# The RWKV gate's eight tiles moved to the wait for the first inverses, with x kept in DRAM meanwhile

## The chip, the cores and the metric

The kernel runs on one core of a Trainium2 chip (TensorE, VectorE, ScalarE, GpSimd and SyncE, which issues most transfers). The metric is the device time of one execution in microseconds, the median of several runs. In the profile PE is TensorE's matmul, PEld its weight load, DVE VectorE, ACT ScalarE, POOL GpSimd, SP SyncE; L2908 is line 2908 of the kernel.

## What is computed

Two blocks of layers over one sequence of 512 tokens with 1024 features: a block of two attention mixers, then a block with an RWKV-7 mixer, a convolutional FFN, windowed attention and a second FFN. All in float32. The change is in the RWKV mixer and its surroundings. Cut to what matters:

```
xr, xw, xk, xv, xa, xg = [x + xx * mu[i] for i in range(6)]
g = sigmoid(xg @ g1) @ g2                       # the gate: 160 features -> 1024
...
S = S * d_t + (S a_t) b_t + v_t k_t ; y_t = S r_t   # a scan over 512 tokens, 16 heads of 64
y = ((y - mean) * rsqrt(var + GN_EPS)) * gn_g + gn_b
bonus = sum(r_h * k_h * r_k, axis=-1, keepdims=True) * v_h
y = y + bonus
mixer = (y * g) @ w_o
x = x + rms_norm(mixer, norm_g[0, 1])
```

## The kernel before

The work is a list of stages, and in each stage every engine has its own stream of instructions, tied by semaphores. `RwkvProject` makes the projections, `RwkvCore` the scan, and an `Output` stage multiplies the core's result with the gate, projects it with `w_o` and adds it to x. At the end of the core all engines wait for each other (`end_stage`).

The residual x rests in SBUF in `env.x`, 4 tiles of 128 tokens x 1024 (2 MB), through the whole kernel. It isn't touched between the norm ahead of the projection and the additions of the `Output` stage (L956).

The core works on eight eighths n = 0 to 7: token tile c = n mod 4, and head group n // 4 (8 heads each). Its work on TensorE is a written-out list, `self.order`: a key such as `("Y", 0)` stands for one step of one eighth. TensorE takes the keys in that order; each key has two of the eight PSUM banks by its place modulo four, and waits until the engine named in `engines` ("A" is ScalarE, "D" VectorE) has taken the result of the key four places before it. ScalarE and VectorE go through the same list and take the keys that are theirs. For one eighth `G1` and `G2` are products that VectorE masks (L3125), `TA` and `Z` are taken by ScalarE, `Y` (L2942) and `OFF` (L2949) put together the inverse of a triangular matrix, and then come `SA0`, `U0`, `S0`, `SA1`, `U1`, `S1` (the state, two chunks of 64 tokens), `R` and `y`, and `T` (L2923), a transpose after which VectorE centres the result (L3091 to L3093). ScalarE squares it (L3012), VectorE reduces the squares (L3100, L3101, a reciprocal), ScalarE takes the root (L3019) and VectorE scales (L3108).

The inverses of 32x32 blocks are made on VectorE by `inverse`, 31 steps of two instructions (L3072, L3074), once for n = 0 to 3 and once for 4 to 7. The first begins in the projection and runs on between VectorE's other work in the core; its result goes to DRAM and is gathered back into another layout by `gather` on SyncE's queue, and `Y` of eighth 0 waits for that. VectorE starts the second inverse once it has `S0` of eighth 0.

The gate is made of eight tiles `("gate", k)`, each of two matmuls of 512 columns: 128 rows of `g2` with `sg[:, 0]` (L2908), and the other 32 rows with `sg[0:32, 1]` (L2909). `sg` is there since the projection. Each float32 matmul shows as two pieces in the profile. In the kernel before they stand at the end of the list, two of them ahead of `T` of eighth 7, and are copied by ScalarE (L3005) into `self.gate`, which is the memory of `k`, needed to the end of the scan.

GpSimd makes the bonus (L3198: v times the bonus of its head; L3200: plus `gn_b`) in the place of v, for one token tile c after another, each followed for c < 3 by the gain (L3204) and the addition (L3207) once VectorE has scaled that tile; for c = 3 VectorE does these two (L3174, L3176). It starts behind `turn` (L3132), which VectorE takes in eighth 6.

Of the kernel before, what the change touches and what calls it, by code (L numbers as in the profile page):

```python
# [7 lines left out]
ALU = mybir.AluOpType  # L8
# [89 lines left out]
class Env:  # L98
# [6 lines left out]
    def __init__(self, nc, ctx, io):  # L105
# [72 lines left out]
        self.stored = self.sem("stored")  # L178
        self.x_added = self.sem("x_added")
# [582 lines left out]
class Output(Stage):  # L762
# [3 lines left out]
    def __init__(self, env, w_out, g_row, oT, o=None, z=None, kd=KD, following=None, before=None, rows=None):  # L766
        super().__init__(env)
        self.rows = rows
        self.o, self.oT, self.kd, self.g_row, self.z = o, oT, kd, g_row, z
        self.before = before  # L770
        self.n = env.outs
        env.outs += 1
        self.ot0, self.tmp0, self.tr0 = env.ots, env.otmps, env.trs
        if o is not None:
            env.trs += KD
            env.ots += KD
        if z is not None:
            env.otmps += KD
        self.lds, self.g0 = load_tokens(env, w_out, 0, D, kd)
        self.y = env.big.rearrange("p (t d) -> p t d", t=NT)  # L780
# [146 lines left out]
    def vector(self, dve, step):  # L927
# [14 lines left out]
        dve.wait_ge(env.g_arrived, 16 * (self.n + 1))  # L942

# [132 lines left out]
class NsaCompressed(Stage):  # L1076


    def __init__(self, env, m, setup, project):
# [23 lines left out]
        self.cmp_ready, self.keys_ready, self.values_ready = env.sem("cmp_ready"), env.sem("cmp_keys_ready"), env.sem("cmp_values_ready")  # L1103
# [5 lines left out]
        self.zeroed = env.sem("cmp_zeroed")  # L1109
# [7 lines left out]
    def tensor(self, pe):  # L1117
# [69 lines left out]
        pe.wait_ge(self.keys_ready, 1)  # L1187
        scores(0)
        for i in range(NT):
# [5 lines left out]
            if i:  # L1195
                pe.wait_ge(self.pT_taken, i)
            else:
                pe.wait_ge(self.values_ready, 1)
# [63 lines left out]
    def vector(self, dve, step):  # L1262
# [25 lines left out]
        for kv in range(2):  # L1288
# [4 lines left out]
                              env.ps[:, 4, 0:GROUPS * NC].rearrange("p (g c) -> p g c", c=NC)).then_inc(self.keys_ready, 1)  # L1293
# [3 lines left out]
        cp.then_inc(self.values_ready, 1)  # L1297
# [1054 lines left out]
class RwkvMemory:  # L2352


    def __init__(self, env):
# [43 lines left out]
        self.bonus_rows = env.take(T, at=slot(6))  # L2399

# [10 lines left out]
        self.gate = self.k  # L2411
# [3 lines left out]
class RwkvProject(Stage):  # L2415
# [229 lines left out]
    def scalar(self, act, step):  # L2645
# [29 lines left out]

        step(nc.scalar.activation(m.keep, env.vec[:, V_B + 24:V_B + 32], ACT.Copy, scale=-1.0, bias=1.0))
# [86 lines left out]
class RwkvCore(Stage):  # L2763
# [11 lines left out]
    def __init__(self, env, m):  # L2775
# [20 lines left out]
        self.order += [("Y", 0), ("OFF", 0)]  # L2796
# [13 lines left out]
        self.order += [("gate", 0), ("gate", 1), ("T", last)] + [("gate", k) for k in range(2, KD)]  # L2810
# [192 lines left out]
    def scalar(self, act, step):  # L3003
# [18 lines left out]
        for key in self.order:  # L3022
# [10 lines left out]
            elif name == "gate":  # L3033
                cp = copy(m.gate[:, n, :], ps[:, 0, :])
# [22 lines left out]
            if name == "gate" and n in (1, 2, 4):  # L3057
                {1: root, 2: square, 4: root}[n](last - 1 if n == 1 else last)
# [20 lines left out]
    def vector(self, dve, step):  # L3079
# [96 lines left out]
        v.tensor_tensor(o, o, m.v[:, NT - 1, :].rearrange("p (k f) -> p k f", f=P), ALU.add)  # L3176

    def gpsimd(self, pool, step):
# [15 lines left out]
        for c in range(NT):  # L3194
            self.wait_ready(pool, "y", NT + c)
            added = m.v[:, c, :]
            heads = added.rearrange("p (h d) -> p h d", d=DH)
            tt(heads, heads, m.bonus[:, c, :].unsqueeze(2).to_broadcast([P, RH, DH]), ALU.mult).then_inc(self.bonus_added, 1)  # L3198
            pool.wait_ge(self.bonus_added, c + 1)
            tt(added, added, m.gn[:, 1, :], ALU.add).then_inc(self.added_ready, 1)  # L3200
            if c < NT - 1:
                pool.wait_ge(self.scaled, NT + c + 1)
                o = m.o[:, c, :, :]
                tt(o, o, m.gn[:, 0, :].rearrange("p (k f) -> p k f", f=P), ALU.mult).then_inc(self.gained, 1)  # L3204
                pool.wait_ge(self.gained, c + 1)
                pool.wait_ge(self.added_ready, c + 1)
                step(tt(o, o, added.rearrange("p (k f) -> p k f", f=P), ALU.add))  # L3207
# [58 lines left out]
def build(nc, io, out):  # L3266
    with ExitStack() as ctx:
# [28 lines left out]
            Output(env, io["w_o_rwkv_2"][0], g[0, 1], rm.oT, rm.o, rm.gate, following=(g[0, 2], fm.u)),  # L3296
# [19 lines left out]
        for stage, after in zip(stages, stages[1:]):  # L3316
            if isinstance(after, DiffProject):
                stage.ahead = after.k[:3]
            elif isinstance(after, RwkvProject):
                stage.shifted, after.norm = after, stage.norm  # L3320
# [75 lines left out]
```

## Time and profile before

| | |
|---|---|
| median of 3 runs | 2237.29 us (2236.55 to 2238.26) |
| span of the profiled execution | 2243.0 us (no other time of it is shown) |
| mean granted clock of TensorE | 0.936 of full speed |
| busy: PE, DVE, ACT, POOL | 92%, 38%, 41%, 41% |
| chain that ended last, by engine | PE 80%, DVE 9%, ACT 3%, POOL 3%, issue 3%, DMA 1% |
| projection, core and output stages around the change | the projection from about 789, the core from about 1043.7, the output stage from 1257.2 us of the span |

Times of rows are microseconds from the start of the span. The granted clock is TensorE's, where 1.00 is 2.4 GHz and 0.50 is 1.2 GHz.

### The profile page before, as it was taken

To read this page: it belongs to the slowest core of one execution; us is meant where nothing else is said; L and a number is where in the kernel's file an instruction comes from. 1 tells how busy PE (TensorE), PEld (TensorE's weight loads), DVE (VectorE), ACT (ScalarE), POOL (GpSimd) and SP (SyncE) were. 2 spreads that over 40 slices of the span, in tenths; PEclk is the share of its full clock that TensorE was granted. 3 is DMA by queue.
4 is the path that set the end of the run, shared out by engine and by line. 5 is a ranking of instruction groups with operands and counts; after the bars stand their busy time and mean duration, and the time that the engine had idled before them with its cause. 6 is when DMAs were issued, how large, how long until landed. Compare 5 with 4: busy or idle time off the path is not lost.

```text
span 2243.0 us, 33578 instructions
## 1 busy us (share of the span) xinstructions
PE 2074.1 (92%) x13582; PEld 1666.0 (74%) x13582; DVE 846.6 (38%) x1809; ACT 927.9 (41%) x1702; POOL 915.1 (41%) x636
## 2 busy tenths in 40 slices
PE   6999899999997888997588999999998999999998
PEld 5898766788865755876577588888887678888887
DVE  2100567230037456057565443334024535334301
ACT  3331477453246544343123354444234645444412
POOL 3332267534456322241012725445434552444542
PEclk9987899999998978898579899999999999999999
DMA  4222100223310221221210223333322122333332
GB/s 146 79 70 76 48 11 2 66 69 94 94 47 29 62 61 41 77 68 41 50 29 19 94 66 94 94 99 109 105 82 76 48 76 65 95 102 96 104 108 80
DMA packets 222393, 161.05 MB, mean 72 GB/s; under 512 B 30663, under 2 KB 205327, under 8 KB 222240
## 3 DMA queue, kind: packets, MB, share of 16 engines
q1 hardware_dynamic: 220048, 151.83, 22.8%
q0 software_dynamic: 2192, 7.07, 1.1%
q8 instruction: 109, 1.79, 0.3%
q14 instruction: 44, 0.36, 0.1%
HBM read 153.64 MB, written 5.24 MB: 71 GB/s over the span
## 4 chain that ended last, share of the span: by engine, by line
PE 80%; DVE 9%; ACT 3%; POOL 3%; issue 3%; DMA 1%; POOLq 1%; SPq 0%; DVEq 0%; PEld 0%; PEldq 0%; ACTq 0%
PE ps L386 15%; PE ps L348 13%; PE ps L350 13%; PE ps L359 13%; PE ps L396 8%; PE ps L1413 2%; PE ps L1426 2%; PE ps L1402 2%; POOL weights_lo L289 1%; DVE ps L949 1%; DVE buffer L956 1%; POOLq L3261 1%; PE ps L1140 1%; PE ps L2965 1%; PE ps L2202 1%
## 5 line engine op out<-in xcount | busy, mean ns | idle before, releaser
L289 POOL TENSOR_TENSOR weights_lo<-buffer,weights_hi 128x1024 fp32r<-128x1024 f32 (+1 forms) x265 | 654.4, 2471 | 981.1 <-ACT weights_hi L278 980.9
L278 ACT ACTIVATE weights_hi<-buffer 128x1024 fp32r<-128x1024 f32 (+1 forms) x265 | 276.2, 1045 | 339.5 <-PE ps L396 284.7
L348 PE MATMUL ps<-u_hi,weights_hi 128*128 128x512 f32 (+1 forms) x752 | 279.3, 379 | 5.6 <-DVE u_lo L703 3.0
L350 PE MATMUL ps<-u_lo,weights_hi 128*128 128x512 f32 (+1 forms) x736 | 274.8, 377 | 0.0
L2000 ACT ACTIVATE buffer<-ps,buffer 128x512 f32<-128x512 f32 x88 | 68.7, 781 | 276.3 <-PE ps L359 276.3
L359 PE MATMUL ps<-u_hi,weights_lo 128*128 128x512 f32 (+1 forms) x752 | 176.5, 377 | 0.0
L2030 DVE SCALAR_TENSOR_TENSOR buffer<-ps,buffer,buffer 128x511 f32<-128x511 f32 x88 | 66.0, 750 | 287.8 <-ACT buffer L2000 287.8
L348 PEld LDWEIGHTS ps<-u_hi,weights_hi 128*128 128x128 f32 x752 | 142.0, 191 | 31.9 <-issue 5.6
L350 PEld LDWEIGHTS ps<-u_lo,weights_hi 128*128 128x128 f32 x736 | 138.4, 188 | 25.5
L359 PEld LDWEIGHTS ps<-u_hi,weights_lo 128*128 128x128 f32 x752 | 136.3, 190 | 25.8
L3005 ACT ACTIVATE buffer<-ps 32x256 f32<-32x256 f32 (+5 forms) x96 | 47.8, 499 | 158.3 <-PE ps L2965 68.3
L386 PE MATMUL ps<-weights_hi,act_hi 128*128 128x512 f32 x352 | 108.8, 390 | 0.5 <-issue 0.5
L386 PE MATMUL ps<-weights_hi,act_lo 128*128 128x512 f32 x352 | 108.4, 389 | 0.0
L1488 POOL TENSOR_SCALAR buffer<-buffer,buffer,buffer 128x512 f32<-128x512 f32 (+3 forms) x128 | 76.8, 612 | 40.8 <-DVE buffer L1368 40.0
L396 PE MATMUL ps<-weights_lo,act_hi 128*128 128x512 f32 x352 | 92.8, 389 | 0.0
L948 DVE RECIPROCAL buffer<-buffer 128x1 f32<-128x1 f32 x24 | 3.9, 161 | 229.5 <-ACT buffer L865 229.5
L348 PE MATMUL ps<-nsa_u_hi,weights_hi 128*128 128x512 f32 x192 | 83.4, 434 | 4.2 <-DVE nsa_u_lo L703 2.4
L1447 ACT ACTIVATE buffer<-buffer,buffer 128x512 f32<-128x512 f32 (+3 forms) x128 | 71.4, 558 | 30.2 <-DVE buffer L1521 29.1
L350 PE MATMUL ps<-nsa_u_lo,weights_hi 128*128 128x512 f32 x192 | 81.3, 424 | 0.0
L348 PE MATMUL ps<-diff_u_hi,weights_hi 128*128 128x512 f32 (+1 forms) x216 | 77.6, 373 | 3.3 <-ACT weights_hi L278 2.2
L386 PEld LDWEIGHTS ps<-weights_hi,act_hi 128*128 128x128 f32 x352 | 65.7, 188 | 15.4 <-issue 2.1
L386 PEld LDWEIGHTS ps<-weights_hi,act_lo 128*128 128x128 f32 x352 | 66.1, 188 | 13.8
(403 smaller groups left out, 4268.2 us busy)
## 6 DMA issues: line engine op xcount, KB each, us to landing
buffer<-in_w_up SPq DMA_DIRECT2D x88, 512.0 KB, 3.8
buffer<-in_w_down SPq DMA_DIRECT2D x44, 512.0 KB, 3.4
buffer<-in_diff_w_in SPq DMA_DIRECT2D x32, 512.0 KB, 4.0
buffer<-in_nsa_w_in SPq DMA_DIRECT2D x28, 512.0 KB, 3.8
buffer<-in_w_rkv SPq DMA_DIRECT2D x24, 512.0 KB, 4.0
buffer<-in_nsa_w_out SPq DMA_DIRECT2D x8, 512.0 KB, 3.6
buffer<-in_diff_w_out SPq DMA_DIRECT2D x8, 512.0 KB, 3.5
buffer<-in_w_o_rwkv SPq DMA_DIRECT2D x8, 512.0 KB, 3.5
```

The lines of the kernel that those rows point to most:

```text
L278: self.nc.scalar.activation(self.part_hi[:, part % self.PARTS, 0:n], self.raw[:, ld % self.RAW, 0:n], ACT.Copy).then_inc(self.hi_ready, 1)
L289: self.nc.gpsimd.tensor_tensor(self.part_lo[:, part % self.PARTS, 0:n], self.raw[:, ld % self.RAW, 0:n], self.part_hi[:, part % self.PARTS ...
L348: nc.tensor.matmul(out, hi[:, k, :], rhs[0][:, k, tokens], start=(k == 0), stop=False)
L350: nc.tensor.matmul(out, hi[:, k, :], rhs[1][:, k, tokens], start=False, stop=False)
L359: mm = nc.tensor.matmul(out, lo[:, k, :], rhs[0][:, k, tokens], start=False, stop=(k == KD - 1))
L386: nc.tensor.matmul(out(i, b), lhs[part][:, index * m + k, i * P:(i + 1) * P], hi[:, k, b * width:(b + 1) * width], start=(index + k == 0 a ...
L396: mm = nc.tensor.matmul(out(i, b), lhs[0][:, index * m + k, i * P:(i + 1) * P], lo[:, k, b * width:(b + 1) * width], start=False, stop=stop)
L1447: nc.scalar.activation(m.p[:, at, 0:n], m.p[:, at, 0:n], ACT.Exp, scale=-1.0, bias=m.nmax[:, at:at + 1], accum_out=m.psum[:, at:at + 1]).t ...
L1488: nc.gpsimd.tensor_scalar(p, p, m.scale[:, at:at + 1], m.gate[:, i, gate:gate + 1], ALU.mult, ALU.mult).then_inc(self.p_scaled, 1)
L2000: nc.scalar.activation(m.conv[:, 2 * (j % 2) + half, :], env.bank(g), ACT.Identity, scale=self.col(2, half, j), bias=self.col(3, half, j)) ...
L2030: step(nc.vector.scalar_tensor_tensor(c[:, 1:T], env.bank(g)[:, 0:T - 1], self.col(1, half, j), c[:, 1:T], ALU.mult, ALU.add))
L3005: copy = lambda dst, src: nc.scalar.activation(dst, src, ACT.Copy)
```

## The change

- The eight `gate` tiles move from the end of the order to the wait for the first inverses: tiles 0 to 3 behind `TA` of eighth 1, then `Z` of eighth 1, then tiles 4 to 7, and behind them `Y` of eighth 0. `T` of eighth 7 is then the last key.
- `self.gate` is no longer the memory of `k`, which is in use then, but that of `env.x`. ScalarE stores x to a DRAM tensor at the start of the projection in one transfer, and waits for it before it copies a gate tile. In the `Output` stage ScalarE loads it back in four transfers, each behind the second of the two gate tiles in its place, and VectorE waits for them ahead of its first addition to x.
- The bonus of token tiles c = 2 and 3 is made right behind `turn`, ahead of c = 0, into free memory (`late`) and not in the place of v, which the scan still reads.
- ScalarE's last root and square steps follow the list, where they followed certain gate tiles.
- In an earlier stage (`NsaCompressed`) two semaphores, `keys_ready` and `values_ready`, become one that counts to 1 and 2, and an unused one goes.

```diff
+        self.x_spilled = self.sem("x_spilled_and_back")
+        self.x_dram = nc.dram_tensor("x_kept", (P, NT * D), F32, kind="Internal").ap()
...
@@ Output.scalar
             nc.scalar.activation(self.oT[0][:, k, :], self.turned(k), ACT.Copy).then_inc(env.oT_hi_ready, 1)
+            if self.x_kept and k % 2:
+                act.dma_start(env.x[:, k // 2, :], env.x_dram[:, k // 2 * D:(k // 2 + 1) * D]).then_inc(env.x_spilled, 16)
...
@@ Output.vector
         dve.wait_ge(env.g_arrived, 16 * (self.n + 1))
+        if self.x_kept:
+            dve.wait_ge(env.x_spilled, 16 * (1 + NT))
...
@@ RwkvMemory
+        late = env.take(2, D, at=slot(6))
+        self.added = [self.v[:, 0, :], self.v[:, 1, :], late[:, 0, :], late[:, 1, :]]
...
-        self.gate = self.k
+        self.gate = env.x.rearrange("p i d -> p (i d)").rearrange("p (k t) -> p k t", k=KD)
...
@@ RwkvProject.scalar
+        env.wait_x(act, self.x_of, NT - 1)
+        act.dma_start(env.x_dram, env.x.rearrange("p i d -> p (i d)")).then_inc(env.x_spilled, 16)
...
@@ RwkvCore.__init__
         self.order = [(name, 0) for name in first] + [("dg", n) for n in range(NT, 2 * NT)] + [(name, 1) for name in first]
-        self.order += [("Y", 0), ("OFF", 0)]
+        self.order[-1:-1] = [("gate", k) for k in range(4)]
+        self.order += [("gate", k) for k in range(4, KD)] + [("Y", 0), ("OFF", 0)]
...
-        self.order += [("gate", 0), ("gate", 1), ("T", last)] + [("gate", k) for k in range(2, KD)]
+        self.order.append(("T", last))
...
@@ RwkvCore.scalar
             elif name == "gate":
+                act.wait_ge(env.x_spilled, 16)
                 cp = copy(m.gate[:, n, :], ps[:, 0, :])
...
-            if name == "gate" and n in (1, 2, 4):
-                {1: root, 2: square, 4: root}[n](last - 1 if n == 1 else last)
+        root(last - 1)
+        square(last)
+        root(last)
...
@@ RwkvCore.gpsimd
-        for c in range(NT):
-            self.wait_ready(pool, "y", NT + c)
-            added = m.v[:, c, :]
-            heads = added.rearrange("p (h d) -> p h d", d=DH)
-            tt(heads, heads, m.bonus[:, c, :].unsqueeze(2).to_broadcast([P, RH, DH]), ALU.mult).then_inc(self.bonus_added, 1)
-            pool.wait_ge(self.bonus_added, c + 1)
-            tt(added, added, m.gn[:, 1, :], ALU.add).then_inc(self.added_ready, 1)
...
+        self.wait_taken(pool, "gate", KD - 1)
+
+        def add_bonus(n, c):
+            heads = lambda x: x.rearrange("p (h d) -> p h d", d=DH)
+            tt(heads(m.added[c]), heads(m.v[:, c, :]), m.bonus[:, c, :].unsqueeze(2).to_broadcast([P, RH, DH]),
+               ALU.mult).then_inc(self.bonus_added, 1)
+            pool.wait_ge(self.bonus_added, n + 1)
+            tt(m.added[c], m.added[c], m.gn[:, 1, :], ALU.add).then_inc(self.added_ready, 1)
+
+        add_bonus(0, 2)
+        add_bonus(1, 3)
+        for c in range(NT - 1):
+            if c < 2:
+                self.wait_ready(pool, "y", NT + c)
+                add_bonus(2 + c, c)
```

## Rows read from the trace of the kernel before

**Rows 1.** Chain that ended last, around the first `Y`: start us, us, what

```profile
1080.44 1.89 DMA buffer<-inverses_turned
1082.47 1.08 PE ps L2942 x32
...
1092.34 0.04 DVE buffer L3156
```

**Rows 2.** Timeline ahead of the first `Y`: start us, us, what, idle before

```profile
1062.53 1.19 DVE L2885 COPY buffer<-ps 32x128 f32<-32x128 f32 x4
...
1070.16 1.97 PE L2934 MATMUL ps<-buffer,buffer 64*64 64x64 f32 x32 [7.32 <-DVE buffer L3125]
```

**Rows 3.** Windows: stretch, us, busy per engine, PEclk, DMA share, GB/s

```profile
1059.80:1063.70 3.90, 1.94 (x8) 1.57 (x8) 3.65 (x12) 0.83 (x1) 0.00 (x0) 0.50 0.00 0
1082.40:1107.00 24.60, 18.23 (x351) 17.01 (x353) 7.98 (x23) 5.16 (x12) 0.00 (x0) 0.50 0.10 17
892.60:900.20 7.60, 7.20 (x9) 2.58 (x9) 6.04 (x7) 4.14 (x7) 3.18 (x2) 0.50 0.00 0
900.20:902.60 2.40, 2.40 (x6) 1.92 (x7) 0.00 (x0) 0.69 (x1) 0.00 (x0) 0.50 0.47 126
1230.50:1237.20 6.70, 6.70 (x112) 5.52 (x110) 3.11 (x6) 1.92 (x4) 3.06 (x2) 0.50 0.01 4
1237.30:1254.00 16.70, 16.66 (x36) 4.81 (x34) 14.07 (x12) 5.00 (x11) 14.86 (x7) 1.00 0.00 0
```

**Rows 4.** Timeline of TensorE: the nearest prices of a gate tile and of `Y`

```profile
893.00 7.19 PE L2475 MATMUL ps<-buffer,buffer 64*128 64x512 f32 x8 [1.52 <-ACT buffer L2708]
...
1236.09 1.68 PE L2908 MATMUL ps<-buffer,buffer 128*128 128x512 f32 x2
...
1238.75 1.13 PE L2908 MATMUL ps<-buffer,buffer 128*128 128x512 f32 x2
...
1198.89 0.69 PE L2942 MATMUL ps<-buffer,buffer 32*32 32x32 f32 x32
```

**Rows 5.** Timeline of GpSimd in the tail of the core

```profile
1221.99 2.35 POOL L3204 TENSOR_TENSOR buffer<-buffer,buffer 128x1024 f32<-128x1024 f32 x1 [13.93 <-DVE buffer L3108]
...
1239.74 1.90 POOL L3198 TENSOR_TENSOR buffer<-buffer,buffer 128x1024 f32<-128x1024 f32 x1
...
1241.72 2.34 POOL L3200 TENSOR_TENSOR buffer<-buffer,buffer 128x1024 f32<-128x1024 f32 x1
...
1252.64 3.20 POOL L3200 TENSOR_TENSOR buffer<-buffer,buffer 128x1024 f32<-128x1024 f32 x1
```

**Rows 6.** Timeline of VectorE, and `T` 7 on TensorE, in the tail

```profile
1209.15 0.17 DVE L3101 TENSOR_SCALAR buffer<-buffer 128x8 f32<-128x8 f32 x1
...
1219.69 0.69 DVE L3091 TENSOR_REDUCE buffer<-ps 128x8 f32<-128x512 f32 x1 [3.04 <-PE ps L2923]
...
1221.23 0.68 DVE L3108 TENSOR_TENSOR buffer<-buffer,buffer 128x512 f32<-128x512 f32 x1
...
1237.56 2.13 DVE L3101 TENSOR_SCALAR buffer<-buffer 128x8 f32<-128x8 f32 x1
...
1240.86 0.66 PE L2923 MATMUL ps<-buffer,buffer 128*128 128x128 f32 x4
...
1248.41 2.40 DVE L3108 TENSOR_TENSOR buffer<-buffer,buffer 128x512 f32<-128x512 f32 x1 [0.31 <-ACT buffer L3019]
...
1250.84 2.81 DVE L3174 TENSOR_TENSOR buffer<-buffer,buffer 128x1024 f32<-128x1024 f32 x1
...
1255.95 1.23 DVE L3176 TENSOR_TENSOR buffer<-buffer 128x1024 f32<-128x1024 f32 x1 [2.30 <-POOL buffer L3200]
```

**Rows 7.** Timeline at the projection's head, and windows behind it and in the output

```profile
791.22 1.23 ACT L2657 ACTIVATE mix_w_hi<-buffer 128x512 fp32r<-128x512 f32 x2 [1.90 <-DVE buffer L2570]
...
794.00:818.00 24.00, 20.04 (x49) 10.19 (x50) 21.05 (x31) 11.95 (x19) 2.35 (x1) 0.65 0.00 0
...
1264.60:1298.00 33.40, 33.40 (x160) 27.66 (x159) 6.62 (x9) 10.13 (x13) 19.29 (x11) 1.00 0.35 112
```

More of the change, by code:

```diff
@@ L762, with __init__ @@
 class Output(Stage):
-    def __init__(self, env, w_out, g_row, oT, o=None, z=None, kd=KD, following=None, before=None, rows=None):
+    def __init__(self, env, w_out, g_row, oT, o=None, z=None, kd=KD, following=None, before=None, rows=None, x_kept=False):
         super().__init__(env)
+        self.x_kept = x_kept
         self.rows = rows
@@ L1102, in __init__ @@
             env.release(self.w1[2 * kv + 1], self.hid_ready, kv + 1)
-        self.cmp_ready, self.keys_ready, self.values_ready = env.sem("cmp_ready"), env.sem("cmp_keys_ready"), env.sem("cmp_values_ready")
+        self.cmp_ready, self.keys_then_values = env.sem("cmp_ready"), env.sem("cmp_keys_then_values")
         self.bias_ready, self.bias_taken = env.sem("cbias_ready"), env.sem("cbias_taken")
@@ L1108, in __init__ @@
         self.o_ready, self.o_taken = env.sem("co_ready"), env.sem("co_taken")
-        self.zeroed = env.sem("cmp_zeroed")
         self.tensor_goes_on = True
@@ L1186, in tensor @@
         project(3)
-        pe.wait_ge(self.keys_ready, 1)
+        pe.wait_ge(self.keys_then_values, 1)
         scores(0)
@@ L1197, in tensor @@
             else:
-                pe.wait_ge(self.values_ready, 1)
+                pe.wait_ge(self.keys_then_values, 2)
             for g in range(GROUPS):
@@ L1292, in vector @@
         nc.vector.tensor_copy(m.kcmp[:, :, 0:NC],
-                              env.ps[:, 4, 0:GROUPS * NC].rearrange("p (g c) -> p g c", c=NC)).then_inc(self.keys_ready, 1)
+                              env.ps[:, 4, 0:GROUPS * NC].rearrange("p (g c) -> p g c", c=NC)).then_inc(self.keys_then_values, 1)
         for j in range(HPG):
@@ L1296, in vector @@
                                        env.ps[0:NC, 5, 0:GROUPS * DH].rearrange("p (g d) -> p g d", d=DH))
-        cp.then_inc(self.values_ready, 1)
+        cp.then_inc(self.keys_then_values, 1)
         take(0)
@@ L3175, in vector @@
         dve.wait_ge(self.added_ready, NT)
-        v.tensor_tensor(o, o, m.v[:, NT - 1, :].rearrange("p (k f) -> p k f", f=P), ALU.add)
+        v.tensor_tensor(o, o, m.added[NT - 1].rearrange("p (k f) -> p k f", f=P), ALU.add)
     def gpsimd(self, pool, step):
@@ L3193, in gpsimd @@
         pool.wait_ge(self.rows, 32)
-        for c in range(NT):
-            self.wait_ready(pool, "y", NT + c)
-            added = m.v[:, c, :]
-            heads = added.rearrange("p (h d) -> p h d", d=DH)
-            tt(heads, heads, m.bonus[:, c, :].unsqueeze(2).to_broadcast([P, RH, DH]), ALU.mult).then_inc(self.bonus_added, 1)
-            pool.wait_ge(self.bonus_added, c + 1)
-            tt(added, added, m.gn[:, 1, :], ALU.add).then_inc(self.added_ready, 1)
[L3201 to L3207, printed above, removed]
+        self.wait_taken(pool, "gate", KD - 1)
[11 more added lines that the diff above has]
+                add_bonus(2 + c, c)
+            pool.wait_ge(self.scaled, NT + c + 1)
+            o = m.o[:, c, :, :]
+            tt(o, o, m.gn[:, 0, :].rearrange("p (k f) -> p k f", f=P), ALU.mult).then_inc(self.gained, 1)
+            pool.wait_ge(self.gained, c + 1)
+            pool.wait_ge(self.added_ready, min(3 + c, NT))
+            step(tt(o, o, m.added[c].rearrange("p (k f) -> p k f", f=P), ALU.add))
     def sync(self, sp):
@@ L3295, in build @@
             core,
-            Output(env, io["w_o_rwkv_2"][0], g[0, 1], rm.oT, rm.o, rm.gate, following=(g[0, 2], fm.u)),
+            Output(env, io["w_o_rwkv_2"][0], g[0, 1], rm.oT, rm.o, rm.gate, following=(g[0, 2], fm.u), x_kept=True),
         ]
@@ L3319, in build @@
             elif isinstance(after, RwkvProject):
-                stage.shifted, after.norm = after, stage.norm
+                stage.shifted, after.norm, after.x_of = after, stage.norm, stage.n
             elif isinstance(after, FfnUp):
```

## Prediction

> **What bounds the kernel now.** I read the chain of work that ended last first, because only a stretch that lies on it can pay. Around the change it runs as follows [rows 1]. The first inverses go out to DRAM and are gathered back; the last transfer the first `Y` needs starts at 1080.44 and takes 1.89 us, so it is in at 1082.33. TensorE takes `Y` of eighth 0 (L2942) at 1082.47, and from there the chain passes through `OFF`, `U0` and `S0` until VectorE has `S0` at 1092.34. VectorE starts the second inverse only behind that `S0`, so whatever delays the first `Y` delays all that follows. The timeline ahead of it [rows 2] shows the wait: VectorE copies the last `dg` from 1062.53 for 1.19 us (1063.72); `Z` of eighth 1 waits for VectorE's masking of `G2` 1, starts at 1070.16 and takes 1.97; otherwise TensorE has nothing until 1082.47. That is the hole into which the gate goes: from 1063.76 to 1082.47, 18.7 us, less 2.0 for `Z`.
>
> The windows [rows 3] I read for one column, TensorE's granted clock: 0.50 is 1.2 GHz, 1.00 is 2.4. The reader should see that it has already fallen to 0.50 in the stretch 1059.8 to 1063.7, before the hole begins, and that it is still 0.50 from 1082.4 to 1107. In the tail, where the gate is made today, it is 1.00.
>
> The tail [rows 5, 6] is bound by neither TensorE nor the gate. It is GpSimd: its last bonus addition ends at 1255.84, VectorE adds the result from 1255.95 for 1.23 us, and the stage ends at 1257.18, three microseconds after the last gate tile.
>
> **Part 1, the gate in the wait: the price of a tile.** At 2.4 GHz a tile, two matmuls of two pieces each, takes 2.11 us: the piece pairs start 1.05 us apart, and the two pieces with 128 rows take 1.13 [rows 4]. Eight take 16.9, and 18.7 - 2.0 = 16.7 are there; at that clock it nearly fits. At 1.2 GHz no whole tile is in the trace. The nearest row from below is L2475: pieces of the same 512 columns and 64 rows, eight in 7.19 us, 0.90 each [rows 4]; four make 3.6 us. From above, twice the tile of 2.11 is 4.2. The first matmul of gate 0 was caught across the change of the clock, at 1.61 us to the next one with some 0.4 of them at 1.00; all at 0.50 it would be about 2.0, and I take 4.0 for a tile.
>
> Which clock? It is at 0.50 when the tiles begin. What did TensorE do before it rose? The L2475 stream kept it busy 7.20 of 7.60 us with 64 rows and left it at 0.50; the L386 matmuls with 128 rows that followed had it up after 2.4 us [rows 3]. In the tail it rose after small-tile work that ended in a first gate matmul, and the gates then merely held it [rows 3, 4]. Half of a gate tile's time goes to the pieces on `w1[0:32]`, with 32 rows; over its whole time it is nearer to L2475 (mean of 128 and 32 is 80) than to L386. So I take 0.50 for all eight.
>
> The Trainium skill, "TensorE: Matmul & The Clock Gate", Part 1, says that 1.2 GHz is the default and that activity of the engine releases it. By that alone the tiles would lift the clock and the change would be worth what the first rival below gives; the L2475 row does not agree with it.
>
> Then gate 0 to 3, `Z`, gate 4 to 7 run in TensorE's order without waiting (the results they need, `dg` 7, `G1` 1 and `G2` 1, are there by 1063.7, 1066.6 and 1070.1): 1063.76 + 8 x 4.0 + 1.97 = 1097.7. Behind them in TensorE's queue stands `Y` of eighth 0, ready since 1082.33. **Delay: +15.3 us** (at 3.6 a tile +12.1, at 4.2 +16.9). ScalarE's eight copies (0.60 each) follow their tile and hide.
>
> **Part 2, what leaves the tail.** GpSimd no longer makes the bonus of tokens c = 2 and 3 there, and `T` of eighth 7 no longer stands behind gate 0 and 1. I follow VectorE [rows 6]. `y` 7 and the reduction behind it are done by 1237.56, when L3101 starts, which took 2.13 instead of the 0.17 of an earlier eighth, until GpSimd's L3207 was done; that stays, and the reciprocal (0.2) ends at 1239.9 as before. `T` 7, which started at 1240.86 and took 0.66, now starts behind `y` 7, near 1237.0, and even at 1.2 GHz (1.1) is ready by 1238.1. From the start of L3091 to the end of L3108, four operations, took 2.22 us in the undisturbed eighth from 1219.69, and GpSimd is now idle there: scaled at 1242.2 instead of some 3.2 later. GpSimd's L3204 and L3207 for c = 2 (2.35 each with 0.07 between, [rows 5]) end at 1247.0, and that is its last work. VectorE's variance again waits for L3204 (1244.7), then square root, and its L3108 again waits for L3207 and ends about 1247.6 (before 1250.8). L3174, which took 2.81 beside GpSimd, is alone now and takes some 1.25, L3176 the same: 1250.2. **Gain: 1257.2 - 1250.2 = -7.0 us.** The bounds are -5.5 (two more collisions of 0.7) and -7.5. TensorE's 16.9 us of tiles leave the tail for nothing, since it was done before the bound was.
>
> **Part 3, the bonus made early.** The two pairs for c = 2 and 3 (1.90 + 2.34 each, [rows 5]) now follow the turn (one pair before 1208.1, so 1203.7), then c = 0: GpSimd is busy until about 1217 instead of 1208.1 (1221.99 less 13.93 idle), and its next work is ready only at 1221.99 [rows 5], so GpSimd itself loses nothing. VectorE does: between 1208.1 and 1217 it has L3154 twice and L3101 once, the kinds that wait while GpSimd computes, and the take of `SA1` stands behind them. L3154, a microsecond before the L3101 at 1209.15 [rows 6], comes just into the gap between two of GpSimd's operations; L3101 has to wait out the rest of a 1.9 us operation, about 1.3; the third about 0.2. **+1.5 us** (0 if both fall into gaps, 4.4 if each waits out a whole operation of about 2.2).
>
> **Part 4, x to DRAM and back.** The store of 2 MB is issued by ScalarE at the head of the projection, where its first copy waited 1.90 us for VectorE [rows 7]; an issue fits there. Its transfer meets a stretch of 24 us in which the DMA share is 0.00 [rows 7]. The four loads of 512 KB go out between ScalarE's copies in the output stage, with a DMA share of 0.35 over 33 us and TensorE busy throughout, and x is wanted only at the first addition, near 1300 [rows 7]. The cover is TensorE's dense matmuls; without it four issues of about 0.4 us would show. **0** (0 to 1.6). The merged semaphores in the compressed stage: same engine, same order, 0.
>
> **Sum.** +15.3 - 7.0 + 1.5 + 0 = **+9.8 us**. The profiled execution has a span of 2243.0 us, 5.7 above the median of 2237.3, and no other time of its own is shown; I add the difference to the median: **2247.1 us**. With all low bounds 12.1 - 7.5 + 0 = +4.6 (2242), with all high ones 16.9 - 5.5 + 4.4 + 1.6 = +17.4 (2255). Every later stretch also starts at another moment against the clock's changes, worth perhaps 2 us either way, so this case alone spans 2240 to 2255.
>
> **Rivals.** *The clock rises among the first tiles* (faster). Say it is up during gate 1. Then TensorE waits for `G2` 1 as before and makes the last six tiles and `Z` by about 1084.2: +1.7. The first `Y`, `OFF` and `Y` would then also run at 1.00, 0.69 against 1.06 to 1.08 and 0.46 less on the chain each [rows 1, 4]: -1.4. Sum 1.7 - 1.4 - 7.0 + 1.5 = -5.2, **2232.1 us**. For it: the gate kept the clock up for 16.7 us once it was up. Against: the clock is down when the tiles start, and L2475. It decides at a mean price of 2.8 us a tile (8 x 2.8 + 2.0 - 18.7 = 5.5 = 7.0 - 1.5), which is three tiles at 0.50 and five at 1.00. *The clock rises halfway*, after gate 4 or 5: +1 to +6 in all, about **2240 us**. *The reload of x is not hidden*: weights or x come late in the output stage, one load of about 4 us on the path on top of the forecast, **2251 us**; against it, 33 us at a share of 0.35 hold 2 MB easily. *The change does nothing*: its two sides would have to cancel, which is the halfway case with four tiles at 1.00.
>
> **Numbers.** Clock low throughout 0.70, with the late reload 0.04 of it; halfway 0.11; clock up early 0.19. The measurement of this kernel tells about 0.2% (4.5 us) from no change. Faster by more: most of the early case, 0.17. Within: the rest of it, a third of the halfway case and the lowest edge of the likeliest, 0.10. Slower: 0.73. The range leaves out at most 2 in 10 only if it takes in the early case: 2231 to 2255 (the early case with a little to spare).
>
> **What the changed profile must show.** Clock at 0.50 in the windows under L2908, each tile about 4 us; the first L2942 near 1097.7 with TensorE instead of the transfer ahead of it on the chain; GpSimd four bonus operations in a row from the turn on; the stage's last L3176 ending 7 us closer behind `y` 7 than before, and at 1250 + 15 + 1.5 = 1267 in absolute time. Wrong it is if the clock column shows 1.00 under the tiles.

## The result, and the profile after

The changed kernel takes 2243.67 us, the median of seven runs (2238.39 to 2249.45), beside 2237.29 for the kernel before on the same chip (2235.38 to 2238.26): ratio 1.0033, with a 95% interval of 1.0020 to 1.0045. It is slower, by some 6.4 us, and the prediction of 2247.1 was 3.4 us too high. The profiled execution took 2248.25 us (span 2246.5), 4.6 above its own median, so it is read below beside a second profile of the same kernel (run a_again, 2246.55 us).

In the new file `gate` is L2919 and L2920, `Y` L2953, the take of `S0` L3169; VectorE's operations of the tail and GpSimd's pair (now L3211 and L3214) have moved by 13 lines, and GpSimd's gain and addition are L3224 and L3227. First the timeline of TensorE around the first `Y`, where [rows 1, 2, 4] stood before.

```profile
1062.09 2.04 PE L2919 MATMUL ps<-buffer,buffer 128*128 128x512 f32 x2 [0.98 <-issue]
1064.06 2.07 PE L2920 MATMUL ps<-buffer,buffer 32*128 32x512 f32 x2
...
1076.08 2.07 PE L2920 MATMUL ps<-buffer,buffer 32*128 32x512 f32 x2
1078.08 1.97 PE L2945 MATMUL ps<-buffer,buffer 64*64 64x64 f32 x32
1079.98 2.07 PE L2919 MATMUL ps<-buffer,buffer 128*128 128x512 f32 x2
1081.99 1.13 PE L2920 MATMUL ps<-buffer,buffer 32*128 32x512 f32 x2
...
1088.31 1.12 PE L2920 MATMUL ps<-buffer,buffer 32*128 32x512 f32 x2
1089.36 0.69 PE L2953 MATMUL ps<-buffer,buffer 32*32 32x32 f32 x32
```

A pair of pieces starts every 2.0 us, a tile every 4.0, for four tiles; then `Z`; and in the middle of the fifth tile the pairs shrink to 1.13 (a pair is two pieces, one line of the fence). The windows say why; the column after the five engines is the granted clock.

```profile
1062.00:1078.00 16.00, 15.91 (x16) 3.99 (x16) 9.38 (x23) 1.95 (x4) 0.00 (x0) 0.50 0.53 135
1078.00:1082.00 4.00, 4.00 (x36) 2.30 (x35) 0.00 (x0) 1.19 (x2) 0.00 (x0) 0.50 0.41 66
1082.00:1089.30 7.30, 7.30 (x15) 2.05 (x14) 0.00 (x0) 1.79 (x3) 0.00 (x0) 1.00 0.09 14
1089.30:1092.30 3.00, 1.86 (x97) 1.61 (x96) 0.00 (x0) 1.89 (x5) 0.00 (x0) 1.00 0.00 0
1092.40:1112.00 19.60, 14.94 (x251) 14.00 (x255) 7.98 (x23) 3.75 (x9) 0.00 (x0) 0.50 0.07 12
```

TensorE was busy for 19.9 of 20.0 us at 0.50 (1.2 GHz) before it was granted 1.00 (2.4 GHz) at 1082.0. The remaining tiles are at 1.05 us a pair. The chain of waits now reaches the first `Y` through the gate (start, length, what), no longer through the transfer.

```profile
1087.33 1.05 PE ps L2919 x2
1088.38 1.05 PE ps L2920 x2
1089.43 0.65 PE ps L2953 x32
```

The last `dg` copy ended at 1061.99 in this profile (before 1063.72), so the delay of `Y` is best counted from there: 27.37 us against 18.75, **+8.6**. `S0` is then taken 8.11 us behind the first `Y` (1097.47), which took 9.87 before [rows 1]: -1.8. The first `Y` and `OFF` still fall into the stretch at 1.00.

The tail, VectorE and then GpSimd (both timelines; before: [rows 5, 6]).

```profile
1248.38 0.69 DVE L3160 TENSOR_TENSOR buffer<-ps,buffer 128x512 f32<-128x512 f32 x1 [1.43 <-PE ps L3010]
...
1249.69 2.13 DVE L3114 TENSOR_SCALAR buffer<-buffer 128x8 f32<-128x8 f32 x1
...
1257.16 2.43 DVE L3121 TENSOR_TENSOR buffer<-buffer,buffer 128x512 f32<-128x512 f32 x1 [0.27 <-ACT buffer L3030]
1259.63 1.22 DVE L3187 TENSOR_TENSOR buffer<-buffer,buffer 128x1024 f32<-128x1024 f32 x1
1260.88 1.23 DVE L3189 TENSOR_TENSOR buffer<-buffer,buffer 128x1024 f32<-128x1024 f32 x1
```

```profile
1254.29 2.34 POOL L3224 TENSOR_TENSOR buffer<-buffer,buffer 128x1024 f32<-128x1024 f32 x1 [2.50 <-DVE buffer L3121]
1256.70 2.34 POOL L3227 TENSOR_TENSOR buffer<-buffer,buffer 128x1024 f32<-128x1024 f32 x1
```

GpSimd's work for c = 2 is its last, L3187 takes 1.22 where it took 2.81, and from `y` 7 (L3160) to the end of the stage there are 13.73 us; before, 1236.24 to 1257.18, 20.94. **-7.2.**

Behind the turn, GpSimd's pairs and VectorE beside them.

```profile
1208.87 1.90 POOL L3211 TENSOR_TENSOR buffer<-buffer,buffer 128x1024 f32<-128x1024 f32 x1 [28.50 <-DVE buffer L3145]
...
1219.58 2.36 POOL L3214 TENSOR_TENSOR buffer<-buffer,buffer 128x1024 f32<-128x1024 f32 x1
```

```profile
1215.44 2.30 DVE L3167 TENSOR_TENSOR buffer<-buffer,buffer 128x256 f32<-128x256 f32 x1
...
1218.38 1.16 DVE L3114 TENSOR_SCALAR buffer<-buffer 128x8 f32<-128x8 f32 x1
```

L3167 takes 0.42 when GpSimd is idle and L3114 0.17, so 2.9 us of waiting beside GpSimd are in these rows. TensorE lost something too, in the middle of the 64 matmuls of a `y` (L3010).

```profile
1210.48 0.75 PE L3010 MATMUL ps<-buffer,buffer 64*64 64x64 f32 x34
1213.43 0.62 PE L3010 MATMUL ps<-buffer,buffer 64*64 64x64 f32 x26 [2.21 <-issue]
```

For 2.21 us it waited for nothing that the profile shows. In the second profile of the changed kernel this pause is absent and only L3114 waits; from the turn to `y` 7 there were 34.1 us instead of 39.5. x behaves as forecast (DMA issues: KB each, median us to landing), and no engine waits for it in the profile.

```profile
x_kept<-buffer ACTq DMA_DIRECT2D x1, 2048.0 KB, 8.1
buffer<-x_kept ACTq DMA_DIRECT2D x4, 512.0 KB, 4.2
```

### The profile page after: what moved, and what is told of

It reads as the page before. It is cut to its first block, busy times and chain, and to the rows that moved or that the text cites. A ratio compares the mean times of both kernels' runs of the same rounds, so it can differ in the third digit from the quotient of the medians.

```text
span 2246.5 us, 33592 instructions
## 1 busy us (share of the span) xinstructions
PE 2082.1 (93%) x13582; PEld 1668.2 (74%) x13582; DVE 849.9 (38%) x1809; ACT 928.1 (41%) x1702; POOL 912.7 (41%) x636
## 4 chain that ended last, share of the span: by engine, by line
PE 83%; DVE 9%; ACT 3%; issue 2%; POOL 2%; POOLq 1%; DMA 1%; DVEq 0%; PEld 0%; PEldq 0%; SPq 0%; ACTq 0%
PE ps L388 15%; PE ps L350 13%; PE ps L352 13%; PE ps L361 13%; PE ps L398 8%; PE ps L1419 2%; PE ps L1432 2%; PE ps L1408 2%; PE ps L2976 1%; DVE ps L956 1%; POOL weights_lo L291 1%; DVE buffer L963 1%; PE ps L1146 1%; PE ps L2208 1%; PE ps L2989 1%
```

## The experiments

There were three comparisons, each on one chip with 35 runs of the kernel before (medians 2236.65, 2239.28 and 2238.92; single runs from 2227 to 2248 us) and 12 runs of every other kernel: e1 to e4; b_again, a_again, e5 and e6; e7 to e10. The ratios and their 95% intervals are those on record; the quotient of the two medians can lie up to 0.0014 from them (e3: 1.0022 beside 1.0008, e4: 1.0044 beside 1.0030), so a difference of less than some 3 us is open whichever is used. One profile of a kernel can lie several us from its median, since the clock falls and rises at other moments each time, so times are read from the ratios and mechanisms from the profiles.

**b_again and a_again: both kernels once more.**

> The kernel before, unchanged, for a second profile of it and as a zero of the comparison. The profiled execution of before (span 2243.0) lies above its own median, so I expect here a shorter stretch somewhere: from the last dg copy to the end of the core's stage 193.5 us in the first profile. Theory A: that stretch differs by several us from execution to execution, because the granted clock falls at different moments of it, and a typical one is shorter than the one read before: 187 to 191 us. Rival: it is the same within 1 us and the difference lies elsewhere. Ratio to before 1.000 within 0.002.

Measured: 2238.61 beside 2239.28, ratio 0.9993 (0.9979 to 1.0007). The stretch from the last `dg` copy to the end of the stage was 190.6 us, 193.5 in the first profile: inside theory A's 187 to 191. From the first `Y` to the turn the mean granted clock was 0.81 and not 0.76, and that part is 2.9 us shorter, as theory A says. The whole execution (span 2242.8) is all the same as long as the first, so the stretch of one profile doesn't give its time.

> The changed kernel, unchanged, beside the others on this chip: 2243 to 2247, ratio 1.002 to 1.004. The gate tiles: 4.0 us each at a granted clock of 0.50 for four tiles and Z, the first Y 27.4 us behind the end of the last dg copy (before 18.7).

Measured: 2246.37 beside 2239.28, ratio 1.0030 (1.0017 to 1.0042), as expected. Tiles and delay repeat exactly: 27.37 us to the first `Y`. The windows of this second profile show the same step from 0.50 to 1.00 behind the same amount of work.

```profile
1065.00:1081.00 16.00, 15.98 (x16) 3.99 (x16) 9.32 (x23) 1.89 (x4) 0.00 (x0) 0.50 0.53 135
1081.00:1084.50 3.50, 3.50 (x35) 2.28 (x34) 0.00 (x0) 1.19 (x2) 0.00 (x0) 0.50 0.39 63
1085.00:1092.30 7.30, 7.30 (x15) 1.99 (x16) 0.00 (x0) 1.79 (x3) 0.00 (x0) 1.00 0.11 18
```

**e1_rows128: the tile's second half with all rows.**

```
+ nc.gpsimd.memset(m.sg[:, 1, :], 0.0).then_inc(self.row_put, 1)
...
- mm = mmul(ps[:, 0, :], w1[0:32, cols], m.sg[0:32, 1, :], start=False, stop=True)
+ mm = mmul(ps[:, 0, :], w1[:, cols], m.sg[:, 1, :], start=False, stop=True)
```

> The changed kernel, but the second half of every gate tile multiplies all 128 rows (rows 32 to 127 of the activations are set to zero by GpSimd, those of the weights hold what the buffer holds; the result of the gate is changed only by products with zero). Columns and number of matmuls stay. Theory A: the clock stayed at 0.50 for four tiles because a tile is mostly pieces with few rows; with 128 rows throughout the granted clock rises inside the first or second tile, tiles then take 2.1 us, the first Y is taken at 1082 to 1085 (changed kernel 1089.4), the time is 2236 to 2240. Rival: rows do not matter, only that TensorE is busy, and the clock rises again at the fifth tile: first Y near 1089, 2243.7 within 3.

Measured: 2236.55 beside 2236.65, ratio 0.9990 (0.9973 to 1.0008): theory A. TensorE's timeline and the windows:

```profile
1063.59 2.05 PE L2921 MATMUL ps<-buffer,buffer 128*128 128x512 f32 x2 [0.99 <-issue]
1065.43 1.52 PE L2922 MATMUL ps<-buffer,buffer 128*128 128x512 f32 x2
1066.79 1.02 PE L2921 MATMUL ps<-buffer,buffer 128*128 128x512 f32 x2
...
1082.14 0.69 PE L2955 MATMUL ps<-buffer,buffer 32*32 32x32 f32 x32 [0.45 <-DMA buffer<-inverses_turned]
```

```profile
1063.50:1066.40 2.90, 2.81 (x4) 1.18 (x4) 2.74 (x6) 0.17 (x1) 0.00 (x0) 0.50 0.87 138
1066.40:1082.00 15.60, 14.11 (x62) 6.16 (x60) 6.65 (x19) 5.05 (x9) 0.00 (x0) 1.00 0.45 123
```

With the same number of matmuls and of columns the clock rose inside the first tile instead of the fifth, the tiles were made by 1081.7, and the first `Y` waits for the transfer again, 18.65 us behind the last `dg` copy. The rows that a tile's second half multiplies are what the two kernels differ in. Four profiles with 32 rows (the changed kernel twice, e2, e4) have 27.3 to 27.4 us to the first `Y`, the one with 128 has 18.65. The Trainium skill, "TensorE: Matmul & The Clock Gate", Part 1, says that 1.2 GHz is the default and that the engine's activity releases it. This run agrees, 2.81 of 2.90 us busy ahead of the rise; the changed kernel agrees only late, 15.91 of 16.00 us busy and still at 0.50.

**e5_between: the tiles where the clock is still up.**

```
- self.order[-1:-1] = [("gate", k) for k in range(4)]
- self.order += [("gate", k) for k in range(4, KD)] + [("Y", 0), ("OFF", 0)]
+ self.order[4:] = [key for k, other in enumerate(self.order[4:]) for key in (other, ("gate", k))]
+ self.order += [("Y", 0), ("OFF", 0)]
```

> The changed kernel, with one gate tile behind each of dg 4 to 7, G1, G2, TA and Z of eighth 1, that is from 1050 on, where the clock is still at 1.00 and TensorE waits some 1.9 of every 3.0 us for VectorE's copies. Theory A (the price of a tile is set by the clock that it starts under): the first tiles cost 2.1 us each and lie in those gaps, the clock stays at 1.00 longer, the first Y is again released by the transfer, some 18.7 to 20 us behind the last dg copy, and the time is that of the run with 128 rows, 2235 to 2239. Rival 1: the tiles delay the dg copies and with them the second inverse; last dg copy 4 or more us later: 2241 to 2245. Rival 2: the clock falls all the same after the first tiles and the others cost 4.0: 2240 to 2244.

Measured: 2236.86 beside 2239.28, ratio 0.9987 (0.9973 to 1.0001). TensorE's timeline and a window:

```profile
1051.48 0.64 PE L2887 MATMUL ps<-buffer 64*64 64x64 f32 x30
1052.05 1.12 PE L2919 MATMUL ps<-buffer,buffer 128*128 128x512 f32 x2
1053.10 1.12 PE L2920 MATMUL ps<-buffer,buffer 32*128 32x512 f32 x2
1054.15 0.69 PE L2887 MATMUL ps<-buffer 64*64 64x64 f32 x32
...
1082.02 1.07 PE L2953 MATMUL ps<-buffer,buffer 32*32 32x32 f32 x32 [7.20 <-DMA buffer<-inverses_turned]
```

```profile
1052.00:1075.00 23.00, 22.82 (x238) 9.96 (x232) 19.96 (x54) 10.44 (x27) 0.00 (x0) 1.00 0.21 39
```

The very same tiles, 32-row halves and all, cost 2.1 us each when they stand between `dg` matmuls at 1.00, and the clock stays there for 23 us; before, it was at 0.50 from 1059.8 [rows 3]. The last `dg` copy ends at 1063.34, so nothing of the second inverse is late, and TensorE has 7.2 us to spare ahead of the first `Y`. Theory A held in all it said, neither rival did.

**e6_spill_only: x to DRAM and back, and the merged semaphores, alone.**

```
+ act.dma_start(env.x_dram, env.x.rearrange("p i d -> p (i d)")).then_inc(env.x_spilled, 16)
+ act.dma_start(env.x[:, k // 2, :], env.x_dram[:, k // 2 * D:(k // 2 + 1) * D]).then_inc(env.x_spilled, 16)
```

> The kernel before, with only x stored to DRAM at the head of the projection and loaded back in the output stage (and the merged semaphores of the compressed stage); gate tiles, gate's place and bonus as before. Theory A, as predicted: 0, ratio 1.000 within 0.002, median 2236 to 2239. Rival (the four loads and the store cost something that no wait of one execution shows): 2240 to 2242, which would explain why the bonus alone is at 2241.5 although it shortens the core's stage.

Measured: 2239.56 beside 2239.28, ratio 0.9997 (0.9985 to 1.0010). Theory A; part 4 of the prediction stands, with an interval of -3.4 to +2.2 us.

**e2_gate_only: the gate moved, the bonus as before.**

```
- add_bonus(0, 2)
- add_bonus(1, 3)
+ for c in range(NT):
+     self.wait_ready(pool, "y", NT + c)
+     added = m.v[:, c, :]
...
```

> The changed kernel with GpSimd's bonus as it was before: added in the place of v, token tile after token tile, those of c = 2 and 3 in the tail. Theory A (of the 12.1 us by which y 7 comes late, 5.1 are the gate tiles, 2.9 VectorE operations that wait for GpSimd's early bonus, 2.2 a stall of TensorE that has to do with the weight loads, the rest the longer stretch at 0.50): y 7 comes 3 to 7 us earlier than in the changed kernel, the tail is 5 to 7 us longer, in sum 2242 to 2246. Rival (early bonus costs nothing; all of the loss is the gate tiles and the loads): y 7 as in the changed kernel, tail 6 longer, 2249 to 2250.

Measured: 2247.39 beside 2236.65, ratio 1.0040 (1.0022 to 1.0057), between theory A's 2242 to 2246 and the rival's 2249. The rival's condition fell: from the last `dg` copy to `y` 7 there are 174.8 us, 7.0 fewer than in a_again and 11.6 fewer than in the changed kernel's first profile, where it wanted no difference. In its profile `y` 7 comes 29.8 us behind the turn, and the tail, 20.63 us, is bound by GpSimd as before, as these rows of VectorE show.

```profile
1247.97 3.25 DVE L3187 TENSOR_TENSOR buffer<-buffer,buffer 128x1024 f32<-128x1024 f32 x1
1255.50 1.22 DVE L3189 TENSOR_TENSOR buffer<-buffer 128x1024 f32<-128x1024 f32 x1 [4.28 <-POOL buffer L3213]
```

So the gate's move alone costs its full 8.7 us (27.38 to the first `Y`) and brings nothing at the end: the tail's -7.2 is the bonus's. The ratio says the same, 1.0040 of 2237 being 8.9 us.

**e3_bonus_only: bonus early, gate in the tail.** The order is that of before, the two early results lie in x's place, x goes to DRAM.

```
- late = env.take(2, D, at=slot(6))
+ late = env.x[:, 2:4, :]
- self.gate = env.x.rearrange("p i d -> p (i d)").rearrange("p (k t) -> p k t", k=KD)
+ self.gate = self.k
...
```

> The bonus of c = 2 and 3 made early as in the changed kernel, gate tiles in the tail and in the place of k as before; x still goes to DRAM and back, and the two early results lie in the place of x. Theory A: first Y as before (near 1082), 1.5 to 3 us lost after the turn to VectorE operations that wait for GpSimd; in the tail 3 to 6 us are won, since GpSimd has less to do and only T of eighth 7 is still behind two gate tiles: 2234 to 2238. Rival (it is the early bonus that lengthens the stretch at 0.50 and costs up to 7 us): 2239 to 2241.

Measured: 2241.55 beside 2236.65, ratio 1.0008 (0.9992 to 1.0023): above theory A's 2234 to 2238 and just above the rival's 2239 to 2241. The first `Y` and the tail are as theory A said; what it didn't have is the stretch between them (part 3 below). The tail is 15.46 us, 5.5 less than before and 1.7 more than with the gate gone: `T` 7 still starts 4.6 us behind `y` 7 (1239.54), behind two gate tiles (TensorE's timeline). VectorE waits 1.57 us for it, and 0.84 and 1.87 for ScalarE's last steps, which follow gate tiles.

```profile
1240.95 1.12 PE L2919 MATMUL ps<-buffer,buffer 32*128 32x512 f32 x2
...
1244.11 0.65 PE L2933 MATMUL ps<-buffer,buffer 128*128 128x128 f32 x4
```

**e9_pairs_for_nothing: the early pairs' cost without their gain.** As e6, with two unused pairs made into x's place behind the turn.

```
+ for c in (2, 3):
...
+     tt(heads(m.unused[c]), heads(m.v[:, c, :]), m.bonus[:, c, :].unsqueeze(2).to_broadcast([P, RH, DH]),
+        ALU.mult).then_inc(self.unused_ready, 1)
+     pool.wait_ge(self.unused_ready, 2 * c - 3)
+     tt(m.unused[c], m.unused[c], m.gn[:, 1, :], ALU.add).then_inc(self.unused_ready, 1)
```

> The kernel before with x stored and loaded back, in which GpSimd makes the two pairs of bonus for c = 2 and 3 right behind the turn as in the changed kernel, into the place of x, and nobody uses them; the bonus that is used is made where it was before. So this is the cost of the early bonus without its gain. Predicted part 3: +1.5 us, 0 to 4.4. Theory A: the runs so far leave +4 to +5 for it (ratio 1.003 measured, less 8.7 for the gate tiles, plus 7.2 of tail, gives 5.2): ratio to before 1.0015 to 1.0025. Rival: 1.5 or less, ratio 1.0007 or less, and the missing 3 us lie elsewhere.

Measured: ratio 1.0007 (0.9994 to 1.0020), medians 2242.43 and 2238.92. The ratio is the rival's bound, the quotient of the medians (1.0016) is theory A's, and the interval reaches into both, so the time decides nothing. Of VectorE's operations behind the turn only one waits in its profile, and `y` 7 comes 34.1 us behind the turn.

```profile
1204.72 0.44 DVE L3165 TENSOR_TENSOR buffer<-buffer,buffer 128x256 f32<-128x256 f32 x1
...
1205.79 1.16 DVE L3112 TENSOR_SCALAR buffer<-buffer 128x8 f32<-128x8 f32 x1
```

**e4_late_release and e7_between_late: one weight load behind the turn instead of three.** In the changed kernel and in the one with tiles in between. The "R" of the second text is `y`: L3010 is the line of `y`, `R` is L2997.

```
- env.release(ld, self.ready, self.at["gate", KD - 1] + 1)
+ env.release(ld, self.ready, len(self.order))
```

> The changed kernel, but the two ring slots of the gate weights g2_2 are given free only at the end of the core's order, as they were in effect before (behind gate 7 in the tail), so the next w_o loads start in the tail and not in one burst behind the turn. Theory A: the stall of 2.2 us of TensorE behind the turn (at 1211.2, while three loads ran) is gone, and y 7 comes 2 to 5 us earlier: 2239 to 2242. Rival 1: the stall has nothing to do with the loads: 2243.7 within 1.5. Rival 2: the late loads now delay the output projection: later than 2245.

> The kernel with the gate tiles one by one between dg, G1, G2, TA and Z, and in addition the two ring slots of g2_2 given free only at the end of the core's order, so that one w_o load instead of three runs behind the turn. Theory A (TensorE's stall of 2.5 us in the second half of R's matmuls behind the turn, in three of five profiles with three loads and in none with one, is an instruction fetch held up by the loads): the stall is gone, the stretch from the first Y to the end of the stage is some 2.5 to 3.4 us shorter than in the run without this (168.5 there), 2233 to 2236, ratio to before 0.997 to 0.998. Rival: stall or none, the median does not move: ratio 0.9987 as there.

Measured: e4 2246.57 beside 2236.65, ratio 1.0030 (1.0013 to 1.0047); e7 2239.58 beside 2238.92, ratio 1.0002 (0.9985 to 1.0019). The pause is shorter in e7 (TensorE):

```profile
1201.81 0.75 PE L3010 MATMUL ps<-buffer,buffer 64*64 64x64 f32 x34
1203.39 0.62 PE L3010 MATMUL ps<-buffer,buffer 64*64 64x64 f32 x26 [0.83 <-issue]
```

and 0.29 us in e4, but neither kernel is faster for it: theory A fell both times. e4's 2246.57 would as a number be rival 2's, later than 2245, but its ratio is the changed kernel's, and the time behind the core is no longer (983.2 us to the end of the span, changed 984.4), so rival 1, the unmoved median, fits best; in e7 too the rival's 0.9987 lies in the interval. With three loads the pause of 2.2 to 2.8 us is in three of five profiles (not in a_again and e2), with one it is at most 0.8 in nine. That the loads cause it is likely but not shown. It isn't the whole loss: e4 has 39.24 us from the turn to `y` 7 almost without it. A share of it in the medians, 1 or 2 us, is inside the intervals.

**e8_between_gate_only: tiles in between, late release, bonus as before.**

> As the run with tiles in between and the late release, but GpSimd's bonus as it was before the change (in place of v, those of c = 2 and 3 in the tail). Gate tiles cost nothing in the wait here, so what is left against before is the value of the gate's leaving the tail. Theory A (the tail is bound by GpSimd, the gate's tiles ran beside it): stretch from y 7 to the end 20.3 to 20.9 us as before, ratio to before 1.000 within 0.0015. Rival (the gate's tiles held the tail too, through T of eighth 7): the tail is 2 or more us shorter, ratio 0.999 or less.

Measured: 2238.04 beside 2238.92, ratio 1.0001 (0.9985 to 1.0016), tail 20.60 us. Theory A: the gate's tiles in the tail cost nothing while the bonus is there.

**e10_one_later: as e7, one of the early pairs behind the pair of c = 1.**

```
- add_bonus(0, 2)
- add_bonus(1, 3)
+ add_bonus(0, 3)
...
+ if c == 1:
+     add_bonus(3, 2)
...
```

> As the run with tiles in between and the late release, but of the two early pairs only that of c = 3 stands behind the turn; that of c = 2 is made into its own place behind the pair of c = 1, where GpSimd waits for eighth 5. Theory A (each pair beside VectorE's small operations costs some 2 us where it stands behind the turn, where the chain has no slack): 1 to 2 us less than with both behind the turn, 2232 to 2235. Rival (the pair costs as much at its new place, or holds up c = 1): the same or 1 to 2 us more.

Measured: 2236.62 beside 2238.92, ratio 0.9990 (0.9973 to 1.0008): above theory A's 2232 to 2235, though 3.0 us below e7 by the medians. Its profile is the shortest of all (span 2234.4; 32.1 us from turn to `y` 7, tail 14.25), but by the intervals it can't be told from e5 or e7, nor from the kernel before.

The stretches of the core in all profiles, in us: from the end of the last `dg` copy to the first `Y`; to GpSimd's first operation behind the turn; to VectorE's `y` 7; to the end of the last addition; their sum; and the ratio.

| kernel | to `Y` | to turn | to `y` 7 | to end | sum | ratio |
|---|---|---|---|---|---|---|
| before | 18.75 | 121.25 | 32.52 | 20.94 | 193.5 | |
| b_again | 18.65 | 118.35 | 33.33 | 20.27 | 190.6 | 0.9993 |
| e6 x alone | 18.64 | 121.28 | 30.09 | 20.94 | 191.0 | 0.9997 |
| changed | 27.37 | 119.51 | 39.51 | 13.73 | 200.1 | 1.0033 |
| a_again | 27.37 | 120.33 | 34.10 | 13.69 | 195.5 | 1.0030 |
| e4 late release | 27.34 | 117.27 | 39.24 | 13.74 | 197.6 | 1.0030 |
| e2 gate only | 27.38 | 117.69 | 29.77 | 20.63 | 195.5 | 1.0040 |
| e3 bonus only | 18.66 | 119.00 | 34.91 | 15.46 | 188.0 | 1.0008 |
| e9 unused pairs | 18.68 | 120.77 | 34.14 | 20.43 | 194.0 | 1.0007 |
| e8 between, gate only | 18.71 | 122.12 | 30.51 | 20.60 | 191.9 | 1.0001 |
| e1 128 rows | 18.65 | 119.22 | 35.16 | 13.72 | 186.8 | 0.9990 |
| e5 between | 18.68 | 119.45 | 35.35 | 13.72 | 187.2 | 0.9987 |
| e7 between, late | 18.68 | 119.31 | 39.28 | 13.86 | 191.1 | 1.0002 |
| e10 one later | 18.76 | 119.46 | 32.08 | 14.25 | 184.6 | 0.9990 |

The means of the first three rows against those of the next three (each three have the same order of the core): +8.7, -1.3, +5.6, -7.0, in sum +6.1 us. By the medians it is +6.4. From the core's end to the end of the span all 14 profiles have 982.8 to 986.0 us (985.8 and 985.6 in the two of the kernel before, 984.4 in both of the changed one), so the output stage behind it hides no part of the loss. Two warnings on the sums: e1, e3, e5 and e10 lie 3.7 to 7.1 us below the mean of the first three rows (191.7), while their ratios say from 2.9 us faster to 1.8 slower, and each has one profile only.

## Why the prediction was near: a size too large and one too small

**The price of a tile: right.** 4.0 us at 0.50, as worked out from 2.11 and L2475; the tiles ran without a gap, `Z` after the fourth, and `Y` of eighth 0 stood behind them. TensorE took the transfer's place on the chain. Two slips in the text change no term of the sum: 8 x 2.8 + 2.0 - 18.7 is 5.7 and not 5.5, and in the first rival nothing waits for `G2` 1, since gate 0 to 3 stand ahead of `Z` and end behind 1070.1.

**The clock under the tiles: wrong from the fifth on.** "So I take 0.50 for all eight" is the step that failed. It rose after four tiles, `Z` and half a tile, 20 us from the first; that is the rival *the clock rises halfway*, which I gave 0.11 and put near 2240, and it is the sign of being wrong that the prediction names, 1.00 in the clock column under the tiles. The term of +15.3 measured +8.7, less 1.3 to the turn, where the first `Y` and `OFF` now run at 1.00. L2475, the row I chose by, was a stream of 7.6 us; it bore out that such work leaves the clock down for a while, and could say nothing of 20 us. The e1 and e5 runs show how near the other side was: with 128 rows, or started while the clock is up, the same eight tiles delay the first `Y` by nothing. The first rival's -5.2 us for that measured -2.2 and -2.9 by the ratios (2237 x 0.0010 and 0.0013), with intervals that reach both -5.2 and 0; the longer stretch of part 3 would account for the rest.

**Part 2, the tail: right in size.** -7.0 forecast, -7.2 in the profile, 13.7 to 13.9 us in every kernel with the gate gone and both pairs early. The steps are right too: behind `y` 7 I had eighth 7 scaled after 6.0, GpSimd done after 10.8 and the stage ended after 14.0 us; they measured 5.8, 10.7 and 13.7. e2 and e8 confirm that the gate's tiles cost nothing there; not foreseen was that with GpSimd's load gone they would (+1.7 in e3, through `T` 7 and ScalarE's steps). The two edits belong together, but only for 1.7 us.

**Part 3, the bonus early: +1.5 was too small.** The waits that I priced are of the size given: VectorE's operations behind the turn took 1.0 us more in a_again, e3, e9 and e10, 1.2 to 1.5 in e1 and e5, 2.3 to 2.9 in the changed kernel, e4 and e7. But from the turn to `y` 7 all eight profiles with two early pairs have 34.1 to 39.5 us (mean 36.5), all five without 29.8 to 33.3 (31.2): +5.2. The times agree in size: e8 and e7 differ in the bonus alone, e7's tail is 6.7 us shorter, and the ratios are equal (1.0001 and 1.0002); by e2 and e4 some 4.7 us of 6.9 are lost again, though e4 differs in the late release too. By each of these the early pairs cost more than the visible waits, though none is sharp by itself. How they do isn't shown. The windows from the turn to `y` 7 (b_again, e6, a_again and the changed kernel, in this order) show the granted clock beside the length.

```profile
1203.63:1236.96 33.33, 28.29 (x655) 25.86 (x652) 16.11 (x29) 9.14 (x18) 14.53 (x7) 0.74 0.01 2
1203.38:1233.47 30.09, 23.91 (x655) 21.86 (x651) 16.42 (x28) 9.26 (x18) 14.61 (x7) 0.89 0.01 3
1212.62:1246.72 34.10, 27.47 (x654) 24.84 (x650) 17.42 (x29) 9.11 (x18) 22.27 (x11) 0.75 0.08 28
1208.87:1248.38 39.51, 30.69 (x654) 27.56 (x650) 19.28 (x29) 9.24 (x18) 23.21 (x11) 0.67 0.07 25
```

At nearly the same clock, 0.74 and 0.75, b_again without early pairs has 33.3 us and a_again with them 34.1: 0.8 us, no more than the wait (e9, at 0.75, has 34.1 too, e3, at 0.77, 34.9). e6, with the same work as b_again and no early pair either, is 3.2 us shorter at 0.89: twice the term that I priced, and no pair in it. In e1 and e5, at 0.86, the pause of 2.5 to 2.8 us and the waits of 1.2 to 1.5 make up most of what they have above e6. The others with two pairs had 0.67 to 0.77, the five without 0.74 to 0.89. So the excess is made of the waits, a pause of TensorE in three profiles, and a longer time at 0.50. Whether the pairs, by making later matmuls late, bring that low clock about, or how much of it is the chance of single profiles, stays open: the kernel before has it too (0.81 and 0.74), and e9, made to price this by itself, left both sizes standing.

**Part 4, x in DRAM: right**, 0 within the measurement (e6).

**The sum.** +15.3 - 7.0 + 1.5 became +8.7 - 1.3 - 7.0 + 5.6. Two errors of the opposite sign, -7.9 for the clock and +4.1 behind the turn, left 3.8 by the profiles and 3.4 by the medians. That the number was so near is luck: with the first error alone it would have been 7.9 us too high, with the second alone 4.1 too low.

No version here beats the kernel before beyond the measurement: e5, e1 and e10 undo the change's loss (0.9987 to 0.9990, against 1.003), and their intervals all reach the kernel before. The bonus's move gives back behind the turn most of what it wins at the end.

## What to carry to other kernels

Filling a wait of TensorE is priced by the clock under the filler: here the same tile cost 4.0 us behind a stretch at 0.50 and 2.1 us in one at 1.00. Try the filler where the engine is still at 1.00, between the small matmuls that leave gaps, before you put it behind them. Read off how long the row you extrapolate from lasted: 7 us at 0.50 do not say what happens in the next 13. And work moved to an idle engine that shares something with a busy one (GpSimd beside VectorE) is not free because it is early: price it by the stretch that it is moved into, not only by the operations that visibly wait.

## What the hardware showed that I had not expected

Eight matmul pairs with 128 and 32 rows in turn, 15.91 of 16.00 us busy, stayed at 0.50, and the clock rose 4 us later, behind `Z` and half a tile; with 128 rows in both halves it rose after 2.9 us. The same mixed tiles held 1.00 for 23 us when they began there. TensorE paused 2.2 to 2.8 us in the middle of the small matmuls of one `y`, with no wait for a semaphore between them, in three of five profiles in which three loads of 512 KB ran then.
